# RMS norms taken by column block, a diagonal product that scales and turns the rows, and a wide first layer, in a two-block transformer kernel on Trainium2

## What is computed

```python
def rmsnorm(x, w):
    y = x * lax.rsqrt(jnp.mean(x * x, axis=-1, keepdims=True) + 1e-6)
    return y * w
# block 1
z = rmsnorm(x, norm1_w) @ w_in             # 12 column blocks of 512, and 16 gate columns
x = x + mixed @ w_out                      # forgetting attention and mLSTM, head norms inside
x = x + peer_ffn(rmsnorm(x, norm2_w), ...) # 16384 experts, w_q first; all experts are streamed
x = rmsnorm(x, final_norm_w)
# block 2
p = rmsnorm(x, mix_norm_w) @ w_in2         # DeltaNet ("dn", "small") and RWKV-7 ("rw") groups
x = x + concat(o_dn, o_rw) @ w_out2        # "out2"
x = x + attention(rmsnorm(x, xa_norm_w) @ wq, rmsnorm(mem, mem_norm_w) @ wk, ... @ wv) @ wo
x = x + square(relu(rmsnorm(x, ffn_norm_w) @ ffn_w1)) @ ffn_w2
return rmsnorm(x, final_norm_w_2)
```

## Time and profile before

| | |
|---|---|
| median of 3 runs | 4199.02 us (4198.34 to 4201.11) |
| the profiled execution | 4199.72 us, its span 4198.0 us |
| granted TensorE clock, mean | 0.933 |
| busy share PE / PEld / DVE / ACT / POOL | 89% / 82% / 57% / 35% / 3% |
| HBM over the span | 153 GB/s |

### The profile page before, as it was taken

How to read it: one execution, slowest core, us unless ns; L and a number is a source line. 1 busy time by engine, 2 the same in 40 slices (tenths; PEclk the granted TensorE clock), 3 DMA queues, 4 the chain that set the end, 5 groups by cost and what they waited for, 6 DMA issues and landing times.

```text
span 4198.0 us, 58456 instructions
## 1 busy us (share of the span) xinstructions
PE 3755.1 (89%) x24282; PEld 3437.4 (82%) x24282; DVE 2403.7 (57%) x2647; ACT 1482.1 (35%) x1182; POOL 138.0 (3%) x159
## 2 busy tenths in 40 slices
PE   8995899999999999999979997648488679999998
PEld 7984799999888899999969896638386568999997
DVE  3545448977677655555556444563734445555555
ACT  3333334355433333333333332121213333333333
POOL 1000000000000000000000001111020000000000
PEclk8998999999999999999989997877678889999999
DMA  4450535566666655555535450000005324555553
GB/s 164 163 196 22 180 142 186 181 221 235 249 241 241 223 197 205 198 193 204 200 140 181 156 186 11 10 0 0 0 0 181 109 81 163 188 190 186 186 188 140
DMA packets 121725, 643.89 MB, mean 153 GB/s; under 512 B 10608, under 2 KB 43760, under 8 KB 48912
## 3 DMA queue, kind: packets, MB, share of 16 engines
q1 hardware_dynamic: 115792, 619.15, 41.8%
q0 software_dynamic: 5824, 23.20, 1.5%
HBM read 614.52 MB, written 27.79 MB: 153 GB/s over the span
## 4 chain that ended last, share of the span: by engine, by line
PE 85%; DVE 10%; ACT 3%; issue 1%; POOL 0%; DVEq 0%; ACTq 0%; PEldq 0%; POOLq 0%
PE pairs L1945 18%; PE pairs L1946 18%; PE pairs L1947 18%; PE quad L1945 6%; PE quad L1946 6%; PE quad L1947 6%; PE quad L2084 2%; PE pairs L2086 2%; PE quad L2076 1%; DVE w_low L1724 1%; PE quad L2014 1%; ACT w_high L951 1%; ACT arena L974 1%; DVE x_t_low L1747 1%; PE quad L2386 1%
## 5 line engine op out<-in xcount | busy, mean ns | idle before, releaser
L1724 DVE TENSOR_TENSOR w_low<-ring,w_high 128x2048 fp32r<-128x2048 f32 (+1 forms) x556 | 1269.3, 2285 | 1131.2 <-ACT w_high L951 1130.6
L951 ACT CAST w_high<-ring 128x2048 fp32r<-128x2048 f32 (+1 forms) x556 | 1055.6, 1900 | 1861.7 <-PE pairs L1947 1376.4
L1945 PE MATMUL pairs<-x_t_high,w_high 128*128 128x256 f32 x2656 | 763.8, 288 | 39.9 <-issue 25.3
L1946 PE MATMUL pairs<-x_t_low,w_high 128*128 128x256 f32 x2656 | 757.1, 285 | 0.0
L1947 PE MATMUL pairs<-x_t_high,w_low 128*128 128x256 f32 x2656 | 757.0, 285 | 0.0
L1945 PE MATMUL pairs<-w_high,act_high 128*128 128x512 f32 x1568 | 612.5, 391 | 9.2 <-DVE w_low L1724 5.8
L1946 PE MATMUL pairs<-w_low,act_high 128*128 128x512 f32 x1568 | 611.8, 390 | 0.0
L1947 PE MATMUL pairs<-w_high,act_low 128*128 128x512 f32 x1568 | 611.6, 390 | 0.0
L1945 PE MATMUL quad<-x_t_high,w_high 128*128 128x256 f32 x1984 | 563.5, 284 | 13.2 <-DVE w_low L1724 7.6
L1946 PE MATMUL quad<-x_t_low,w_high 128*128 128x256 f32 x1984 | 563.3, 284 | 0.0
L1947 PE MATMUL quad<-x_t_high,w_low 128*128 128x256 f32 x1984 | 563.2, 284 | 0.0
(11 more groups left out here) (458 smaller groups left out, 3600.2 us busy)
## 6 DMA issues: line engine op xcount, KB each, us to landing
ring<-pu SPq DMA_DIRECT2D x128, 1024.0 KB, 4.8
ring<-pv SPq DMA_DIRECT2D x128, 1024.0 KB, 4.8
ring<-f SPq DMA_DIRECT2D x128, 1024.0 KB, 4.8
ring<-win SPq DMA_DIRECT2D x48, 1024.0 KB, 4.8
ring<-dn SPq DMA_DIRECT2D x32, 1024.0 KB, 4.8
ring<-rw SPq DMA_DIRECT2D x24, 1024.0 KB, 4.8
ring<-wout SPq DMA_DIRECT2D x16, 1024.0 KB, 4.8
ring<-wq SPq DMA_DIRECT2D x16, 1024.0 KB, 4.8
```

What stands on the lines that cost most here:

```text
L951: nc.scalar.copy(WH[s % 2][:, 0:w], flat(ring[s])[:, 0:w]).then_inc(ev["split_high"], 1)
L1724: v.tensor_tensor(WL[s % 2][:, 0:w], flat(ring[s])[:, 0:w], WH[s % 2][:, 0:w].bitcast(F32), ALU.subtract).then_inc(ev["split_low"], 1)
L1945: mm(out, stat[0], mov[0], start=start, stop=False, skip_group_check=True)
L1946: mm(out, stat[0], mov[1], start=False, stop=False, skip_group_check=True)
```

## The change

1. **Norms by column block.** As each 512-column block of X becomes final, VectorE multiplies it by the norm's weights (`weigh`; the weight row is now loaded over all partitions), and ScalarE squares it. After the last block only its own squares remain; `total` adds the partial sums.
2. **Scale by a diagonal product.** `diagonal` makes a 128 × 128 diagonal of the reciprocal roots for each token row; `turned_rows` multiplies the weighted rows by it, as ordinary matmuls, which scales and turns at once. Banks now hold both token halves of a k-group in turn, so the product's first slot waits for two banks only (`ready`); banks 4 to 7 are turned after the first slot. ScalarE and VectorE split straight from PSUM (`rows`), without the multiplication between.
3. **Block 1's final norm and block 2's first** are made from one pass: sums of squares of X and of X × w, with a root of each.
4. **Memory norm inside out2**, with its own tiles `MXH`, `MXL`; xk and xv read these, and X's rows are turned inside xk and xv.
5. **The gates' matmuls** stand after the first win product.
6. **Wide first layer** (`first_wide`) in the 15 interleaved PEER blocks and the FFN: high weights × [high | low] activations as one 512-column matmul into four banks, and low weights × high as one of 256. VectorE adds the halves into `HID`, and ScalarE's activation works there in place.
7. **The final norm** of the last two column halves on two engines, stored by half rows; X is loaded and waited for by token row.

```diff
+        XTB = XT_[:, :].rearrange("p (w k t) -> p w k t", w=2, k=KT)
+        def first_wide(pe, mm, n, before=None, following=None):
+            for s in range(4):
...
+                for k in range(4):
+                    kt = 4 * s + k
+                    for m in range(4):
+                        cols = slice(m * P, (m + 1) * P)
+                        mm(PQ[:, m, :], wh[:, k, cols], XTB[:, :, kt, :], start=(kt == 0), stop=False, skip_group_check=True)
+                        ins = mm(PQ[:, m, 0:T], wl[:, k, cols], XTH[:, kt, :], start=False, stop=(kt == KT - 1),
+                                 skip_group_check=True)
+                ins.then_inc(used, 1)
...
@@ PEER block, VectorE
-                for k in range(1, 6):
+                for k in range(1, 5):
                     low(n + k, k % 4)
+                dve.wait_ge(used, n + 4)
+                v.tensor_reduce(HIDB[1 - par].rearrange("p (m t) -> p m t", m=4), PQ[:, :, :].rearrange("p m (w t) -> p m t w", w=2), AX.X, ALU.add
+                                ).then_inc(ev["peer_summed"], 1)
+                low(n + 5, 1)
@@ PEER end, VectorE
+            def ended(nb):
+                dve.wait_ge(ev["dve_free"], d0 + 4 * (EB - 1) + nb + 1)
+                cols = slice(BLK * nb, BLK * (nb + 1))
+                o.done(v.tensor_tensor(A1X[:, :, cols], X[:, :, cols], rep(FNW1[:, cols], NT), ALU.mult), ev["ax_ready"])
+                o.tell(v.tensor_tensor(SCN[:, :, cols], A1X[:, :, cols], rep(MIX2W[:, cols], NT), ALU.mult), ev["dn_weighted"])
@@ out2, VectorE
             lows("out2", 0, range(4))
+            lows("out2", 1, (0,))
+            dve.wait_ge(ev["squared"], 2 + 8 + 16 + 2)
+            dve.wait_ge(ev["mem_w_in"], 16)
+            for t in range(NT):
+                o.tell(v.tensor_tensor(MEMX[:, t, :], MEMX[:, t, :], FINW, ALU.mult), ev["mem_weighted"])
+            add_pair("out2", 0)
+            diagonal()
+            lows("out2", 1, (1, 2))
+            dve.wait_ge(ev["xa_w_in"], 16)
+            weigh("xa_weighted", 0, FINW, XWX)
...
@@ out2, ScalarE
+            highs("out2", 0, range(4))
+            highs("out2", 1, (0, 1))
+            roots()
+            act.wait_ge(ev["mem_in"], 32)
+            squares(MEMX, slice(0, D), av(20480, NT, D), [SS[:, t:t + 1] for t in range(NT)])
+            act.wait_ge(ev["squared"], o.n[id(ev["squared"])])
+            o.tell(nc.scalar.activation(RS, SS, ACT.Sqrt, scale=1.0 / D, bias=EPSC), ev["norm_root"])
+            highs("out2", 1, (2,))
...
@@ xo to ffn, VectorE
+            total(2 + 8 + 16 + 2 + 8 + 8)
+            diagonal()
+            rows(6, range(8))
+            lows("ffn", 0, (1,))
             two_dve(dve, o, v, "ffn", FB, low)
@@ helpers
+            def turned_rows(i, src, banks):
+                for n in banks:
+                    if n >= 4:
+                        pe.wait_ge(ev["rows_low"], 8 * i + n - 3)
+                    ps = PP[:, (n % 4) // 2, n % 2, :] if i == 6 else PQ[:, n % 4, :]
+                    for m in range(4):
+                        kt = 4 * (n // 2) + m
+                        ins = mm(ps[:, m * P:(m + 1) * P], src[:, n % 2, kt * P:(kt + 1) * P], DIAG[:, n % 2, :],
+                                 start=True, stop=True)
+                    ins.then_inc(ev["turned"], 1)
+            def turn_into(i, weighted, count, src, name, feat):
+                pe.wait_ge(ev["diag"], [1, None, 2, 3, 4, 5, 6][i])
+                pe.wait_ge(ev[weighted], count)
+                turned_rows(i, src, range(4))
+                product(name, 0, 1, feat, before=ready(i),
+                        following=lambda s: turned_rows(i, src, range(4, 8)) if s == 0 else None)
+            def weigh(name, j, w, dst):
+                dve.wait_ge(ev["dve_free"], o.n[id(ev["dve_free"])])
+                cols = slice(BLK * j, BLK * (j + 1))
+                o.tell(v.tensor_tensor(dst[:, :, cols], X[:, :, cols], rep(w[:, cols], NT), ALU.mult), ev[name])
+            def total(done):
+                dve.wait_ge(ev["squared"], done)
+                o.done(v.tensor_reduce(SS, SQ, AX.X, ALU.add), ev["summed"])
+            def diagonal():
+                diagonal.n += 1
+                dve.wait_ge(ev["norm_root"], diagonal.n)
+                o.done(v.reciprocal(RSTD, RS))
+                for t in range(NT):
+                    ins = v.tensor_scalar(DIAG[:, t, :], ID, RSTD[:, t:t + 1], None, ALU.mult)
+                o.done(ins, ev["diag"])
```

More of the change, by code:

```diff
@@ L671, in two_act @@
             block(base + 8 * blocks - 12, blocks - 1, 1)
-            for s in range(4):
-                high(base + 8 * blocks - 4 + s, s)
         def peer_act(act, o, high):
@@ new lines, in rows, with squares @@
+            def rows(i, banks, dst=XTH):
+                for n in banks:
+                    act.wait_ge(ev["turned"], TURNED[i] + n + 1)
+                    nc.scalar.copy(dst[:, 4 * (n // 2):4 * (n // 2) + 4, (n % 2) * P:(n % 2 + 1) * P], bank(i, n)
+                                   ).then_inc(ev["rows_high"], 1)
+            def squares(src, cols, junk, sums):
+                for t in range(NT):
+                    act.wait_ge(ev["squared"], o.n[id(ev["squared"])] - 1)
+                    o.tell(nc.scalar.activation(junk[:, t], src[:, t, cols], ACT.Square, accum_out=sums[t]), ev["squared"])
@@ L1050, in _ @@
             peer_act(act, o, high)
-            stage2_act(act, o, half, freed, sums, high, highs, split_rows)
+            stage2_act(act, o, half, freed, norm, high, highs)
         def mlstm_dve(dve, o, v):
@@ new lines, in stage2_dve @@
+            lows("out2", 2, (1, 2))
+            rows(4, (0, 1), (MXH, MXL))
+            lows("out2", 2, (3,))
+            rows(4, (2, 3), (MXH, MXL))
+            lows("out2", 3, (0,))
+            rows(4, (4, 5), (MXH, MXL))
+            add_pair("out2", 2)
+            lows("out2", 3, (1,))
+            weigh("xa_weighted", 2, FINW, XWX)
+            rows(4, (6, 7), (MXH, MXL))
+            lows("out2", 3, (2, 3))
+            lows("xk", 0, (0,))
+            add_pair("out2", 3)
+            weigh("xa_weighted", 3, FINW, XWX)
@@ L1811, in _ @@
                     freed(ins)
+                if j == 0:
+                    gates()
                 if j < 11:
@@ L1900, in _ @@
             peer_dve(dve, o, v, low)
-            stage2_dve(dve, o, v, half, freed, turn_out, turn_out_y, scale_rows, add_pair, low, lows)
+            stage2_dve(dve, o, v, half, freed, norm, turn_out_y, add_pair, low, lows)
         def mlstm_pe(pe, mm):
```

541 lines of the change are left out of this document (349 added, 192 removed).

## The result

The changed kernel takes 4137.31 us in the median of four runs (4136.78 to 4138.50), the kernel before took 4198.78 beside it (4198.34 to 4201.11). The ratio is 0.9852, 95% interval 0.9840 to 0.9864. That is 62 us faster; I forecast 96, 4104, and the range ended at 4131. The profiled execution took 4137.72 us, its span is 4135.6.

What follows compares the result with a forecast made beforehand. TensorE was taken as the bound: its pitch where weights stream, standstill at norms between stages. Savings 26 + 6 + 10 + 17 + 28 + 4 + 5 = 96 from 4199.7 gave 4104 us; range 4085 to 4131.

Steps and rivals of the forecast that it cites:

- diagonal products: At each norm's turning: a diagonal product of 128 columns costs what a transpose does, 0.11 us warm, 0.21 cold.
- the wide matmul: First layers of 31 PEER and FFN blocks: a triple takes 0.347 us instead of 0.36, saving 26 us over 1984.
- the start: From kernel start to the second input product, norm1 and gates included: 6 us saved, from -3 to 11.
- the end: After the last block: shorter squares, final scales on two engines and half-row stores save 5 us.
- out2 to xq: Norms before xk and xq go, saving 44 us; out2's stall, clock and turned memory rows cost 16: net 28.
- norm2: Norm before the query product (wq): first slot at T+8.3 instead of T+20.3, 1.8 us inserted, 10 saved.
- ffn: From the end of xo to the second FFN block: 50 us against 54.0, 4 saved.
- mix2: Two norms before dn from one set of sums: first slot at T+10.2 instead of T+31.0, 17 us saved.
- rival 4: out2 stall shorter, or diagonal products keep the clock up at four cold restarts, 2 to 3 us each: 4090; chance 0.11.
- The wait in out2: In out2 TensorE stalls 9.6 us on a low split queued behind the memory rows' squares and weighings.
- Rival 3: In-order queues push low splits past their due time; 0.5 us over per streamed block gives 4120; chance 0.12.
- Rival 5: Joining sum in 31 first layers slow from its 1 KB stride; at 7 us the kernel takes 4225; chance 0.02.

Runs made afterwards that it cites:

- plain_turn: The changed kernel with each product against the scaled diagonal replaced by a transpose, the scaling left out: 4119.4 us, ratio 0.9806.
- start_order: The changed kernel with ScalarE copying the first four turned banks before the second slot's split, VectorE splitting the first slot after two banks: 4135.3 us, ratio 0.9841.
- grouped: The changed kernel with first_wide's matmuls ordered, per k tile, as four of 512 columns, then four of 256: 4135.8 us, ratio 0.9841.
- narrow: The changed kernel with first_wide's 512-column matmul again two of 256 columns, the joining sum on VectorE kept: 4148.2 us, ratio 0.9877.
- joined_gates: The changed kernel with mem_early, ffn_low, start_order, grouped, gates_turned and rows scaled on VectorE in pieces, then transposed, all together: 4082.8 us, ratio 0.9718.
- mem_early: The changed kernel with the memory norm's squares and weighings in out2 moved one weight slot forward: 4128.0 us, ratio 0.9826.
- ffn_low: The changed kernel with VectorE's low split of the second FFN slot between the FFN norm's first and last four banks: 4134.2 us, ratio 0.9839.
- gates_turned: The changed kernel with the gates computed turned, 16 weight columns in the array and 256 tokens moving: 4127.3 us, ratio 0.9825.

## Why the prediction missed

The direction, the places and most mechanisms were right; two terms were mis-sized, and they come to nearly the whole miss: 4137.7 − 4104 = 33.7, of which the second instruction of the diagonal products is 19.3 (plain_turn) and the wide matmul 12.7 (26 − 13.3). The smaller errors are some 12 us on one side (the rest of the start, the small steps, the end) and some 10 on the other (warm first slots, xo); that they cancel to 1.7 is luck.

*The price of a diagonal product.* The step that failed is "A diagonal product of 128 columns costs what a transpose does", for which I read "12 ordinary ones take 1.50 us warm, 0.11 each"; a diagonal product took 0.224 us, twice that. The line in the earlier trace rows counts instructions. The code behind it makes 32 products, and the trace has 64 records for them, so its 12 instructions are 6 products. One count of records against products would have shown it. For the transposes, 16 records are 16 transposes. So the page's groups have to be divided by the loop's count, and not only the time by the records. The Trainium skill ("FP8 and Floating Point Precision", section "TensorE Precision Notes") says that true FP32 takes four passes through the array. The trace agrees: 128 columns at the 2.4 GHz level are 0.053 us, four times that is an estimate of 0.213, and the two instructions take 2 × 0.112. By that page the term would have been nearly right, and I had not weighed it. That section says nothing of transposes, which take one instruction of 0.11 in the same type.

It hid in several rows of the table: of out2 to xq (28 forecast, 21.2) it explains 6.3, of norm2 3.2, of the start 2.7, of ffn 2.9. That norm2 and mix2 still came out within 1 us is luck, a second error of the other sign. I had counted on a cold first slot. The first slots of the query product and of dn ran warm, as these stretches of the changed kernel show (columns as in the earlier trace rows):

```profile
525.60:531.40 5.80, 5.80 (x50) 5.80 (x49) 3.52 (x3) 0.58 (x1) 0.00 (x0) 1.00 0.17 27
2146.30:2152.10 5.80, 5.80 (x51) 5.80 (x50) 3.58 (x3) 0.59 (x1) 0.00 (x0) 1.00 0.18 25
```

Before, the clock in the query product's first slot was 0.51. Half of rival 4 had said this, that diagonal products leave the clock up. But plain_turn, which only transposes, also has the first slot at 1.00 (521.6 to 527.4). So it is not the kind of instruction. What changed in both is that the turning is one unbroken stretch of TensorE right ahead of the product, where the old one stopped for each bank. The start fits this: there the turning was unbroken too, but 3.7 us passed between it and the first slot, and that slot ran at 0.50 until 31.9; in start_order, with 1.2 us between, it ran at 1.00. I infer this from the traces; no run was made to separate it.

*The wide matmul.* The step "a 512-column matmul has a pitch of 0.227" was taken from a row in which 512 follows 512, and "0.12" from one in which 256 follows 256. In the pair they take 0.236 and 0.117. The bounds were 0.227 and 0.24, the truth is nearly the upper one, and I had chosen the lower on the ground that "weight loads and columns are those of that row". The saving was a difference of 0.013 between two numbers of 0.36; an error of 0.006 in a pitch was half of the largest term. The order of matmuls (grouped) gives back 5 us of it. The 2.5 ns a matmul of the Trainium skill ("TensorE: Matmul & The Clock Gate", section "Wait — 56ns, not 53.3ns?") would have given 5 us by estimate; the 13.3 measured lie between that and the 26 of my rows.

*The start.* I forecast 6 and lost 2. The first slot was 1.5 late, of which plain_turn removes 0.8; ScalarE's second high split, which I had seen in its queue and priced into the "about 25", cost 2.4; the second half's turning took 3.5 and not 1.8; the gates took 17.0 and not 14; and the clock stood at 0.50 until 76.3, 3.8 us into the second product. All these errors have the same sign. I had given the term a range of −3 to 11, and it lies in it.

*What held.* The sum on VectorE is free (2.29 us, as its row said; no TensorE wait on it in steady blocks; narrow shows it from the other side). The new chain at a norm: the turning starts 4.6 us after wout (forecast 4.8). The wait in out2: 9.07 (9.6). xv to xq: 2.6 (2.5). FFN: gaps of 3.7 and 9.9 (3 to 4, and 10). The end is 1.2 short: 3.8 (5). All of these were sums of durations from rows of the same form; the two that failed were pitches moved into a neighbourhood or an instruction type that their row didn't have.

*The range.* It took in the whole loss of the wide term (4130) but not two terms wrong in the same direction. The diagonal product had no upper bound at all, because I took its price as known. Its two-sided bound, one to two instructions, would have added some 19 us.

Two rivals are closed. Rival 3 (queues past their due time in the streamed blocks) did not occur: the block period is 44.39 = 22.60 + 21.79, the second layer is at its old 21.79. Rival 5 (a slow sum) neither: 2.291.

Open: why a pair takes 6 ns more than its two parts, of which the order gives back about 3; and 4 to 5 us lost in PEER and the small steps, which I see only as a shift of the low-clock stretches and did not test.

## What to carry to other kernels

Before an instruction's row is used as a price, divide the group's records by the number of operations that the code issues: an fp32 product that replaces an fp32 transpose costs twice its time on TensorE, and scaling the rows in pieces on an engine with room costs next to nothing. When a saving is the small difference of two pitches, take the pitch from a row with the same neighbours or give the term the full width of its bounds. And when a norm is spread over the blocks of the product before it, look at the order in the queues, which here gave 21 of the 56 us that joined_gates gained (mem_early, ffn_low and start_order): put the new work ahead of the split for which its data are already there, not behind it.

## What I had not expected of the hardware

- A plain fp32 product of 128 columns is two instructions in the trace, 0.112 us each at full clock and 0.213 at half; an fp32 transpose of the same tile is one of 0.11.
- A moving operand in two pieces 4096 columns apart costs the same as one piece: 0.236 both. Mixing 512 and 256 columns costs 6 ns a pair, in rows of four about 3 ns.
- A matmul of 16 moving columns with 128 columns in the array takes 0.111 us warm, as much as one of 128. With 16 columns in the array and 256 moving it takes 0.113 (gates_turned, 5.33 us over 47). The Trainium skill ("TensorE: Matmul & The Clock Gate", section "LDWEIGHTS (loading the stationary operand)") says that loading takes as long as the number of stationary columns asks, about 107 ns for 128. The rows agree at full clock; at half clock it took 0.213, so the figure doubles with it.
- The clock fell in the midst of the 16-column matmuls, at 59.2, and stood at 0.50 for 17.1 us, though TensorE was busy throughout:

```profile
59.20:76.30 17.10, 17.10 (x82) 17.10 (x82) 2.17 (x6) 2.02 (x4) 0.00 (x0) 0.50 0.19 62
```

With 256 columns moving (gates_turned) it stayed at 1.00 through the gates. So the busy share doesn't tell the clock: TensorE is busy for 100% of this stretch at 0.50, as it is in a cold restart such as 3393.5 to 3399.2 in the earlier trace rows, but here no gap stood before it.
